# An encoder layer on one core: the gated unit's input and the first branch's gate in seven products each, among the state-space heads

## The reference

```python
h = rmsnorm(x, norm_mix)
xa, ya, uv, zc, xbc, dtc, gates = split(h @ w_in)
y_a = rglru(xa) * gelu(ya)                 # first branch, ya is its gate
u, v = split(gelu(uv))                     # second branch, the gated unit
y_b = u * (causal(w_s) @ layernorm(v) + b_s)
y_c = ssd(zc, xbc, dtc)                    # third: 16 state-space heads in 8 pairs
merged = sum_k sigmoid(gates_k) * (y_k @ w_k_proj)
x = x + merged @ w_out                     # then cross attention, then 32 experts, top 2
```

## Time and profile before

| | |
|---|---|
| median of 3 runs | 969.76 us (968.07, 969.76 and 2809.84) |
| the profiled execution | 968.18 us, its span 966.4 us |
| PE busy | 821.9 us (85%) |
| PEld busy | 654.7 us (68%) |
| DVE busy | 341.5 us (35%) |
| ACT busy | 190.3 us (20%) |
| POOL busy | 324.5 us (34%) |
| HBM read | 283.08 MB, 294 GB/s over the span |
| mean granted clock of TensorE | 0.954 |

### The profile page before, as it was taken

How to read it: one execution, slowest core, us unless ns; L and a number is a source line. 1 busy time by engine, 2 the same in 40 slices (tenths; PEclk the granted TensorE clock), 3 DMA queues, 4 the chain that set the end, 5 groups by cost and what they waited for, 6 DMA issues and landing times.

```text
span 966.4 us, 18382 instructions
## 1 busy us (share of the span) xinstructions
PE 821.9 (85%) x8068; PEld 654.7 (68%) x8068; DVE 341.5 (35%) x861; ACT 190.3 (20%) x354; POOL 324.5 (34%) x169
## 2 busy tenths in 40 slices
PE   8999999999999999999999996666765656676665
PEld 7999988889999999999887653333433333333332
DVE  2888323647263434343213352212112122121112
ACT  2521138731231000102012111011110111101102
POOL 5876630038998879996300000000000000000000
PEclk9999999999999999999999999889889899889897
DMA  9854534443464344447597999999999999999994
GB/s 311 253 176 176 178 128 162 144 153 110 175 218 174 138 160 149 167 173 264 222 430 308 414 425 428 426 428 425 429 425 429 425 429 427 427 427 427 426 429 197
DMA packets 62405, 285.32 MB, mean 295 GB/s; under 512 B 6692, under 2 KB 11640, under 8 KB 50168
## 3 DMA queue, kind: packets, MB, share of 16 engines
q1 hardware_dynamic: 58056, 280.84, 73.0%
q10 hardware_dynamic: 4272, 3.32, 1.2%
HBM read 283.08 MB, written 1.06 MB: 294 GB/s over the span
## 4 chain that ended last, share of the span: by engine, by line
PE 59%; DMA 25%; SPq 7%; another core or an unknown queue 3%; DVE 2%; ACT 2%; POOL 1%; issue 1%; ACTq 0%; DVEq 0%; POOLq 0%
PE bank L1664 31%; DMA blk<-in_w_down_dram 9%; PE bank L1562 7%; SPq L418 6%; DMA params<-in_w_down_dram 5%; DMA ring<-in_w_down_dram 5%; DMA ring<-in_w_gate_up_dram 5%; PE bank L1659 5%; PE bank L1931 4%; PE bank L1953 2%; PE bank L1630 1%; SPq L453 1%; PE bank L1900 1%; PE bank L1818 1%
## 5 line engine op out<-in xcount | busy, mean ns | idle before, releaser
L1664 PE MATMUL bank<-blk,ring 128*128 128x128 f32 x1840 | 213.3, 275 | 0.4 <-POOL blk L546 0.4
L1664 PEld LDWEIGHTS bank<-blk,ring 128*128 128x128 f32 x1840 | 209.3, 192 | 1.9 <-issue 1.8
L1931 PE MATMUL bank<-ring,cbm 128*32 128x256 f32 x1088 | 78.6, 437 | 46.6 <-DMA ring<-in_w_gate_up_dram 46.6
L1417 DVE TENSOR_TENSOR cbm<-bank,gq 128x256 f32<-128x256 f32 x32 | 13.6, 425 | 251.0 <-PE bank L1900 251.0
L1931 PEld LDWEIGHTS bank<-ring,cbm 128*32 128x32 f32 x1088 | 39.9, 122 | 77.8 <-issue 53.8
L1562 PE MATMUL bank<-blk,ring 128*128 128x256 f32 x384 | 85.4, 381 | 0.8 <-DVE blk L1343 0.8
L1562 PEld LDWEIGHTS bank<-blk,ring 128*128 128x128 f32 x384 | 72.1, 190 | 11.6 <-DVE blk L1343 1.2
L510 POOL TENSOR_TENSOR ring<-ring 128x1024 f32<-128x1024 f32 x20 | 47.4, 2368 | 97.1 <-DVE dec L1141 75.6
L1931 PE MATMUL bank<-blk,cbm 128*32 128x256 f32 x768 | 53.3, 424 | 25.4 <-DMA blk<-in_w_gate_up_dram 25.2
L1664 PE MATMUL bank<-ring 128*128 128x128 f32 x608 | 71.0, 275 | 0.0
L1664 PEld LDWEIGHTS bank<-ring 128*128 128x128 f32 x608 | 69.4, 192 | 0.0
(11 more groups left out here) (342 smaller groups left out, 1070.0 us busy)
## 6 DMA issues: line engine op xcount, KB each, us to landing
ring<-in_w_gate_up_dram SPq DMA_DIRECT2D x34, 2048.0 KB, 49.8
blk<-in_w_gate_up_dram SPq DMA_DIRECT2D x24, 2048.0 KB, 49.5
ring<-in_w_in_dram SPq DMA_DIRECT2D x19, 2048.0 KB, 7.8
ring<-in_w_down_dram SPq DMA_DIRECT2D x18, 2048.0 KB, 49.5
blk<-in_w_down_dram SPq DMA_DIRECT2D x10, 2048.0 KB, 50.7
params<-in_w_gate_up_dram SPq DMA_DIRECT2D x6, 2048.0 KB, 50.6
ring<-in_w_kv_dram SPq DMA_DIRECT2D x4, 2048.0 KB, 8.3
params<-in_w_down_dram SPq DMA_DIRECT2D x3, 2048.0 KB, 49.8
```

Of the source, the lines that this page charges most:

```text
L1417: v.tensor_tensor(xeN, gu_bank(p)[:, T:2 * T], gq[:, :], ALU.mult).then_inc(sem["xn3_ready"], 1)
L1664: last = mm(out_[:, f], wt[:, k, f * P:(f + 1) * P], xt[:, k, :], start=k == 0, stop=k == 3)
L1931: last = mm(gu_bank(p)[c * WIN:(c + 1) * WIN, 0:2 * SEG], xe[:, xin, 4 * j + k, :], w[:, k, :, c, :], start=4 * j + k == 0, stop=4 * j + k ...
```

## The change

The four slabs of u and ya are computed in seven products each, as the others, instead of eight plain units, and the heads stand among them: after slab u0 heads(0), heads(1) behind the fourth product of u1, heads(2) after u1, heads(3) inside ya0, heads(4) after it, heads(5) inside ya1, heads(6) after it. GpSimd makes the four sums for each of the four slabs. VectorE folds each slab; ScalarE copies its first product and applies one Gelu to each folded half (`gelu`). exps(0) and exps(1) move ahead of the sixteen exponentials of the first branch. The sums and copies get new places where tiles are taken, and with them new waits: the first sum for ya0 waits for weights(2) (`w_ready` of 3), the first for ya1 and for gA0 until the slab before has ended its sixth product, the copy for ya1 until exponents(7) is done. GpSimd no longer waits for weights(6).

```diff
-    order += ["wst0", "u0", "u1", "y0", "u2", "y1", "u3", "y2", "ya0", "y3", "ya1", "y4", "ya2", "y5",
-              "ya3", "y6"]
+    order += ["wst0"] + seven("u", 0) + ["y0"] + around(seven("u", 1), "y1") + ["y2"]
+    order += around(seven("ya", 0), "y3") + ["y4"] + around(seven("ya", 1), "y5") + ["y6"]
...
-            two, one = (5, 8) if j < GATE else (10, 2) if j == GATE else (11, 14)
+            two = 5 if j <= U1 else 10 if j <= GATE else 11
+            one = {GATE: 2}.get(j, 8 if j < U1 else two if j < GATE else 14)
...
-            home = block(8 if j < GATE else 2 if j == GATE else 14)
+            home, c = {YA0: (5, 1024), YA1: (7, 0), GATE: (2, 1024)}.get(j, (8 if j <= U1 else 14, 1024))
...
-                if j == GATE:
-                    pool.wait_ge(sem["w_ready"], KD - 1)
-                if j not in (0, GATE, EARLY):
+                if j == YA0:
+                    pool.wait_ge(sem["w_ready"], 3)
+                elif j in (YA1, GATE):
+                    pool.wait_ge(sem["product"], 6 * j)
+                elif j not in (0, EARLY):
                     pool.wait_ge(sem["product"], 6 * (j - 1) + 2)
...
-                if j not in (0, GATE, EARLY):
+                if U1 <= j < GATE:
+                    pool.wait_ge(sem["product"], 6 * j + 2)
+                elif j not in (0, GATE, EARLY):
                     pool.wait_ge(sem["product"], 6 * (j - 1) + 6)
...
+                if j == YA1:
+                    act.wait_ge(sem["cs_taken"], KD)
...
+            exps(0)
+            exps(1)
+            mids("u", 0)
             act.wait_ge(sem["c_ready"], 1)
...
-            for i in range(1, 4):
-                evac(f"u{i}", uT, ACT.Gelu_apprx_tanh)
-                exps(i + 1)
-            for i in range(4):
-                evac(f"ya{i}", yaT, ACT.Gelu_apprx_tanh)
-                if i < 3:
-                    exps(5 + i)
+            gelu("u", uT, 0)
+            exps(2)
+            mids("u", 1)
+            exps(3)
+            gelu("u", uT, 1)
+            exps(4)
+            mids("ya", 0)
+            exps(5)
+            gelu("ya", yaT, 0)
+            exps(6)
+            mids("ya", 1)
+            exps(7)
+            gelu("ya", yaT, 1)
...
             weights(0)
+            dve.wait_ge(sem["a2_ready"], 1)
+            v.tensor_scalar(a2T, a2T, 1.0, None, ALU.min).then_inc(sem["a2_min"], 1)
+            fold("u", 0, columns(uT, 0))
             skip(0)
             exponents(2)
...
             for i in range(2, KD):
                 weights(i)
+                if i == 2:
+                    fold("u", 1, columns(uT, 1))
+                if i in (4, 6):
+                    fold("ya", i // 2 - 2, columns(yaT, i // 2 - 2))
                 scan(1)
                 skip(i)
...
-            dense("u0", hT)
-            for i in range(1, 4):
-                dense(f"u{i}", hT)
-                heads(i - 1)
-            for i in range(3):
-                dense(f"ya{i}", hT)
-                heads(3 + i)
-            dense("ya3", hT)
+            strassen("u", 0, hT, TA, 0)
+            heads(0)
+            strassen("u", 1, hT, TA, 0, middle=1)
+            heads(2)
+            strassen("ya", 0, hT, TA, 0, middle=3)
+            heads(4)
+            strassen("ya", 1, hT, TA, 0, middle=5)
             heads(6)
```

66 lines of the change are left out of this document (34 added, 32 removed).

## The result

The changed kernel takes 981.22 us (median of 978.24, 981.21, 981.23 and 982.08), the kernel before, on the same chip, 970.46 us. The ratio is 1.0115, 95% interval 1.010 to 1.013: slower by 1.1%, less than the 2% that the forecast set as its line between "same" and "slower". The forecast was 974.0 with a range of 966.0 to 979.5, so the sign is right and the time lies 1.7 us above the range. The profiled execution took 981.21 us, its span 979.3 us, 12.9 more than that of the kernel before.

What follows compares the result with a forecast made beforehand. TensorE was taken to bound the kernel up to the transfer-bound expert stage. Stalls of 11.0 less 6.0 gained make 5.0 us; 968.2 + 5.0 = 973.2, plus 0.8, gives 974.0 us, range 966.0 to 979.5.

Steps and rivals of the forecast that it cites:

- The waits: TensorE's stalls for VectorE's weights at heads(1), (2), (3), (5), (7) and for GpSimd's sums in ya0: 11.0 us.
- heads(1) 0.5: Stall at heads(1) behind VectorE's fold of u0, skip(0), exponents(2), batch statistics and weights(1): 0.5 us, the least certain term.
- heads(7) 3.9: Stall at heads(7) behind the gating unit, with weights(7) held by GpSimd's sums for gA0: 3.9 us.
- The walk along the borders of the sums: Timing VectorE's exponents and weights beside GpSimd's sums, one operation passing at each border between sums: stalls of 11.0 us.
- Rival 1: At exponents and weights the holding does not bite; only 1.4 at heads(2) and 1.5 in ya0 remain: 965.9 us, chance 0.15.
- Rival 2: Two VectorE operations pass at each border of GpSimd's sums; heads(7) gets 2.3 us back: 971.7 us, chance 0.12.
- The gain without waits: TensorE's work in the rebuilt stretch falls from 66.95 to 61.0 us: 6.0 us gained (5.3 to 6.7).
- the heads unit: One heads unit among TensorE's slabs costs 0.9 us (bounds 0.8 and 1.0), seven of them 6.3.
- Behind it nothing more is lost: From the first gate slab on, 5.0 us later, everything is the old profile, shifted one for one to the end.
- rival 3: One more border missed at heads(1), (4) or (6), 2.35 us each, or heads(7)'s pause halves the clock: 978.7 us, chance 0.12.
- The 0.8 that the forecast added for the median: Added to the 973.2 us summed from one execution, because other undisturbed runs lay up to 1.6 above: 0.8 us.
- Rival 4: The transfer-bound expert stage absorbs the delay: 969 us, chance 0.03.

Runs made afterwards that it cites:

- e5: Changed kernel with GpSimd's sums for ya0, ya1 and gA0 cut to two columns of each 256 (wrong results); 969.09 us, ratio 0.9993.
- e4: Changed kernel with 7, 6 and 17 unread products filling TensorE's waits ahead of heads(3), heads(5) and heads(7); 974.43 us, ratio 1.0039.
- e10: Changed kernel with 30 one-column products at the start of TensorE's stream in place of five 128-column ones; 977.39 us, ratio 1.0088.
- e12: e8 with weights(2) ahead of VectorE's product of gxT and a2T, and e10's edit at the start of TensorE's stream; 968.53 us, ratio 0.9986.
- e8: Changed kernel with only u in seven products, ya plain and the gate slab's sums at the old wait; 970.21 us, ratio 1.0003.
- e1: Changed kernel with GpSimd's first sum for gate slab gA0 also waiting until weights(7) is done; 978.57 us, ratio 1.0078.
- e2: e1 plus, for ya0 and ya1, the third sum waiting for the exponents and the fourth for the weights; 975.69 us, ratio 1.0058.
- e6: e2 with VectorE's last two scans done while it waits for heads(6) and heads(7); 978.92 us, ratio 1.0092.
- e9: e2 with the gate slab's first two sums at the old, earlier wait and in another place, the third after weights(7); 974.8 us, ratio 1.0055.
- e3: Kernel before the change plus eight unread GpSimd sums, four beside the loop of heads(3) and four beside that of heads(5); 978.82 us, ratio 1.0078.

## Why the prediction was off

**The waits: right.** Named were heads(1) 0.5, heads(2) 1.4, ya0's sums 1.5, heads(3) 2.1, heads(5) 1.6, heads(7) 3.9, together 11.0 us. As idle time of TensorE they were about 0.2, 1.24, 0.98 (0.68 and 0.30), 1.90, 1.62 and 4.28, together 10.2. As delays from one start to the next, which is what the forecast counted, they were 0.2, 1.3, 1.5, 2.0, 1.7 and 4.35, together 11.0 (a product behind a wait takes 2.05 us instead of 1.95). The walk along the borders of the sums found the place, the releaser and the size of each; that the sum fits to a tenth is partly luck, since heads(1) came out lower and heads(7) higher. Rival 1 (no holding) is out: exponents(4) took 2.01, 2.37, 0.34 and 2.37 us, weights(7) 7.2 us in all where 1.40 are its work, and e5 shows that without the sums the waits at heads(3), (5) and (7) vanish. Rival 2 (two operations pass at each border) is out as well, though at one border of each group two did end: in exponents(4) and in weights(7) the second operation was held to its border and the third passed in the gap behind it. Four operations took three borders, and the wait at heads(7) was longer than forecast, not shorter.

**The gain without waits: 0.6 us too large.** The sum said 6.0 (5.3 to 6.7), e5 gives 5.4. The term that was small is the heads unit: the forecast took 0.9 us for each of seven, but among products of the scheme of seven it costs 1.0 (two products with heads(0) between them start at 161.05 and 165.63, 4.58 us for what is 3.58 without it).

**The clock: the step that failed.** The sum carried each wait at its own length, at full clock, and "Behind it nothing more is lost". The half clock stood in rival 3 only, as a doubt about the pause at heads(7), and was not worked out from rows. Measured from rows at either level: 6.76 against 5.62 behind heads(3), 10.73 against 9.20 in the gate slab, and the two heads units 1.26 and 1.48 us long instead of 0.81 each; 1.1 + 1.5 + 0.5 + 0.7 = 3.8 us. e4, with the waits kept and the clock full, has a stretch 3.7 us shorter. The Trainium skill ("TensorE: Matmul & The Clock Gate", "Part 1: The HAM clock gate") has the rule that an idle TensorE is clocked down. The traces agree in part: the granted clock was 0.59 and 0.57 around heads(3) and heads(7) of the changed kernel, but 1.00 behind the same 1.90 us of wait in e10.

The forecast could have priced it. The trace of the kernel before has, in the expert stage, 20 waits of 2.65 to 3.06 us ahead of a unit of 32 records (L1931). Behind three of them the unit took 1.93 us, behind the other seventeen 2.51 to 3.64; the mean of all is 2.98, about 1.0 us for each wait. An estimate from that for four waits at the heads would have been some 4 us more, 978, though these rows are of another stage and say nothing of waits under 2.65 us.

The stretch by its terms: 11.0 of waits and 3.8 of clock, less 5.4 gained, make 9.4 lost, against 11.0 - 6.0 = 5.0 in the forecast.

**The tail: not foreseen.** Everything behind the stretch was taken to move as a block. It does, up to the experts (9.5 us later at their start), but the end has the gap of 2.42 us, and the span is 12.9 us longer. Between the medians the difference is 10.8, since the profiled execution of the kernel before is 2.3 us under its median. The 0.8 that the forecast added for the median does not cover this. With the waits as forecast, the clock's 3.8 us and this gap are most of the distance from 974.0 to 981.2. That the gap goes with e10's edit is shown by e10, where nothing else was changed; that the place of TensorE's later instructions decides it fits e4 and e12 and is argued; by what mechanism stays open, since nothing in a profile names it.

**Rival 4** (absorbed by the experts) is out: 9.5 us at their start are 10.1 at the last down product (955.33 before, 965.43 after).

**What the change could have been.** The forecast took the change as one block. Its two halves differ: for u the sums lie beside work of VectorE that is early enough, and 1.3 us stay (e8), 2.6 with weights(2) moved (e12). For ya the sums lie beside exponents and weights, and the place taken for them moves the gate slab's sums as well; each way tried to put them elsewhere (e1, e2, e6, e9) moved the wait to ya's own products or to pA0.

## What to carry to other kernels

A count of saved products is worth only what the helpers leave of it: lay the helper's sums beside the other engine's short operations and walk the borders, since here four short operations between SBUF tiles took three borders between sums of 2.4 us. Then add to the waits of a TensorE that was dense until there what the clock may take behind them, here 1.6 to 3.8 us on 10 us of waits, priced from rows of the trace in hand. Cheap products in the waits saved 1.5 us here behind the longest of them; more is not shown. If a wait is taken away, look at once for the next user of the same helper; and compare profiles from the start of the stretch, since a kernel's start and end differ by 2 us for reasons that have nothing to do with the edit.

## What the runs showed of the hardware

- A wait of 1.9 us of a TensorE that had been dense drew the lower clock behind it in two profiles (the changed kernel and its repeat: 6.76 and 7.25 us for 48 records of 5.62) and not in two others (e1 and e10, 5.62), with the same wait. Longer ones split too: 2.26 us in e1 did (48 records in 7.61), 2.25 in e2 did not, 3.0 and 3.1 in e3 and 3.7 in e6 did. One of 4.3 us did so in all three profiles that have it (80 records in 10.73, 11.24 and, in e10, 10.82 us instead of 9.20; in e10 the heads unit ahead of them was still at full clock), and the waits of 1.2 to 1.65 us at heads(2) and heads(5) in none. So the clock's part of a loss can't be read from the length of the wait alone.
- A gap of 2.42 us ahead of TensorE's last small product, which no row explains, went away with 30 tiny products at the very start of its program (e10). It was there with 2.0 to 3.0 us in eight profiles and absent in six.
- The holding is mutual: VectorE's 128 x 2048 product stretched a sum of GpSimd from 2.36 to 4.40 us, and was itself stretched from 2.29 to 4.26 when it came second.
